# FoX/mLSTM/PEER encoder step: the forget sums of the later attention move from a product of their own into a 65th row of the keys

## The reference

```python
def fox_attend(q, F_q, q_pos, k, v, F_k):
    s = jnp.einsum('blhd,bshd->bhls', q, k).astype(jnp.float32) * (A_HEAD_DIM ** -0.5)
    s = s + F_q[..., None] - F_k[:, :, None, :]
    mask = jnp.arange(k.shape[1])[None, :] <= q_pos[:, None]
    p = jax.nn.softmax(jnp.where(mask, s, NEG), axis=-1).astype(v.dtype)
    return jnp.einsum('bhls,bshd->blhd', p, v)
```

## Time and profile before

| | |
|---|---|
| median of 3 runs | 4564.17 us (4562.99 to 4566.83) |
| profiled execution | 4577.09 us, span 4575.2 us |
| granted TensorE clock, mean | 0.86 |
| PE busy | 3507.8 us (77%) |
| DVE busy | 3136.7 us (69%) |
| POOL busy | 1793.7 us (39%) |
| ACT busy | 773.3 us (17%) |
| DMA | 1227 MB, 268 GB/s over the span |

### The profile page before, as it was taken

How to read it: one execution, slowest core, us unless ns; L and a number is a source line. 1 busy time by engine, 2 the same in 40 slices (tenths; PEclk the granted TensorE clock), 3 DMA queues, 4 the chain that set the end, 5 groups by cost and what they waited for, 6 DMA issues and landing times.

```text
span 4575.2 us, 37157 instructions
## 1 busy us (share of the span) xinstructions
PE 3507.8 (77%) x11412; PEld 2052.7 (45%) x11412; DVE 3136.7 (69%) x6095; ACT 773.3 (17%) x1322; POOL 1793.7 (39%) x1567
## 2 busy tenths in 40 slices
PE   7767786895588656966649666799898989998970
PEld 2434554553363443534535356544444444444430
DVE  1132203111688887996779889788888888888896
ACT  1141001101230322122222134200000000000000
POOL 0000000000566664762212221366666666666664
PEclk9888697898799877987769878799999999999995
DMA  6102121234999887996457665799999999999996
GB/s 263 61 27 87 65 78 38 85 99 149 327 356 345 311 303 286 404 358 223 144 160 248 211 195 172 251 410 409 409 400 404 398 403 408 399 406 405 402 389 241
DMA packets 436027, 1227.29 MB, mean 268 GB/s; under 512 B 40188, under 2 KB 162172, under 8 KB 431748
## 3 DMA queue, kind: packets, MB, share of 16 engines
q0 software_dynamic: 221184, 805.40, 46.7%
q1 hardware_dynamic: 107648, 209.81, 13.1%
q10 hardware_dynamic: 107024, 210.04, 12.4%
HBM read 1158.71 MB, written 66.39 MB: 268 GB/s over the span
## 4 chain that ended last, share of the span: by engine, by line
DVE 21%; DMA 18%; PE 15%; issue 10%; POOL 9%; ACT 2%; SPq 0%; DVEq 0%; POOLq 0%; ACTq 0%
DMA expert_rows<-in_expert_u,expert_index 12%; POOL expert_rows L2792 9%; PE ps_all L2202 6%; DVE acc L3018 3%; DVE expert_rows L3002 2%; DVE keep L2474 2%; PE ps_all L1610 2%; PE ps_all L2225 1%; DVE half_index L2882 1%; PE ps_all L1861 1%; PE ps_all L2501 1%; DVE half_index L2879 1%; PE ps_all L1824 1%; DMA expert_rows<-in_expert_v,expert_index 1%; DVE half_best L2881 1%
## 5 line engine op out<-in xcount | busy, mean ns | idle before, releaser
L2792 POOL DMA_INDIRECT expert_rows<-in_expert_v,expert_index x768 | 891.0, 1160 | 926.6 <-DVE acc L3018 425.1
L2792 POOL DMA_INDIRECT expert_rows<-in_expert_u,expert_index x768 | 892.1, 1162 | 693.5 <-DVE acc L3018 278.5
L3002 DVE CUSTOM_DVE_ANT_0 expert_rows<-expert_rows,h_rows_sb 128x1024 f32<-128x1024 f32 x768 | 923.3, 1223 | 168.7 <-DMA expert_rows<-in_expert_u,expert_index 158.6
L3018 DVE SCALAR_TENSOR_TENSOR acc<-expert_rows,weights,acc 128x1024 f32<-128x1024 f32 x756 | 937.1, 1289 | 31.7 <-DMA expert_rows<-in_expert_v,expert_index 28.8
L2521 PE MATMUL ps_all<-branchT,side 128*128 128x512 f32 x1536 | 714.7, 617 | 109.8 <-DVE side L2486 109.5
L2512 PE MATMUL ps_all<-hT,branchT 128*128 128x384 f32 x2048 | 704.5, 499 | 54.8 <-ACT side L2456 40.4
L2512 PEld LDWEIGHTS ps_all<-hT,branchT 128*128 128x128 f32 x2048 | 398.2, 195 | 369.5 <-issue 141.1
L2521 PEld LDWEIGHTS ps_all<-branchT,side 128*128 128x128 f32 x1536 | 300.5, 198 | 481.8 <-issue 326.3
L2202 PE MATMUL ps_all<-hT,side 128*128 128x384 f32 x1152 | 393.6, 499 | 38.1 <-ACT hT L2283 20.9
L2202 PEld LDWEIGHTS ps_all<-hT,side 128*128 128x128 f32 x1152 | 223.5, 196 | 196.6 <-ACT hT L2283 21.5
L2501 PE MATMUL ps_all<-keep 128*128 128x128 f32 x768 | 150.8, 365 | 86.4 <-DVE keep L2474 57.3
(11 more groups left out here) (405 smaller groups left out, 4356.3 us busy)
## 6 DMA issues: line engine op xcount, KB each, us to landing
branchT<-in_expert_uT ACTq DMA_DIRECT2D x128, 512.0 KB, 7.1
branchT<-in_expert_vj ACTq DMA_DIRECT2D x128, 512.0 KB, 9.6
w_mod_ring<-in_w_mod SPq DMA_DIRECT2D x12, 2048.0 KB, 9.9
gate_rows<-branchT ACTq DMA_DIRECT2D x12, 2048.0 KB, 9.9
keep<-gate_rows ACTq DMA_DIRECT2D x32, 768.0 KB, 12.4
side<-in_w_blk SPq DMA_DIRECT2D x40, 512.0 KB, 6.0
expert_rows<-in_expert_u,expert_index POOLq DMA_INDIRECT x768, 12.7
expert_rows<-in_expert_v,expert_index POOLq DMA_INDIRECT x768, 11.2
```

Source lines behind the costliest of these rows:

```text
L2792: pool.indirect_dma_start(rows[:, r % ROWS, :], None, io[table], bass.IndirectOffsetOnAxis(ap=eidx[:, q % 3, k:k + 1], axis=0)).then_inc(r ...
L3002: dve.tensor_tensor_reduce(rows[:, r % ROWS, :], rows[:, r % ROWS, :], h2[:, :], 1.0, 0.0, ALU.mult, ALU.add, dot[:, j, k:k + 1]).then_inc ...
L3018: dve.scalar_tensor_tensor(own, rows[:, r % ROWS, :], wgt[:, j, k:k + 1], own, ALU.mult, ALU.add).then_inc(row_used, 1)
```

## The change

The forget sums become row 64 of each head's keys, and the queries get a row of ones there. Rows 65 to 127 of both are zeros. The product of `head_rows` with `negF` goes. The keys of a pair, before one tile of 128 rows, are now two (one a head) with 64 rows used, and take twice the columns; the queries move into the columns of `hbT` that the chunk's mLSTM fills later. Each pair is loaded with 7 transfers (before: 8 in chunk 0, 6 in chunk 1), among them one `negF` row for each head from SBUF. The memsets become four large ones in chunk 0 and one in chunk 1, and now SP waits for them before it loads the first two pairs, and PE doesn't. The planned cost of an attend beat in `side_beats` becomes 0.75 a tile plus 0.8.

```diff
--- before.py
+++ after.py
@@ -1700,8 +1700,9 @@
         self.haT, self.hbT = branchT[:, 0:4, :], branchT[:, 4:8, :]
         self.causal, self.causalT = masks[:, P:2 * P], masks[:, 2 * P:3 * P]
         self.head_rows = masks[:, 4 * P:12 * P].rearrange("p (h t) -> p h t", h=AH)
-        pair = lambda a: (a[:, 4:8, 0:2 * P], a[:, 0:4, 0:2 * P], a[:, :, 2 * P:3 * P])
-        self.pair = (pair(branchT), pair(hT))
+        own = slice(tiles[0] * P, tiles[0] * P + LW)
+        pair = lambda j, a: (self.hbT[:, 2 * j:2 * j + 2, own], a[:, :, 0:2 * P].rearrange("p (h n) t -> p h n t", h=2), a[:, :, 2 * P:3 * P])
+        self.pair = (pair(0, branchT), pair(1, hT))
         self.prob = side[:, 0:2 * SEQ].rearrange("p (j t) -> p j t", j=2)
         self.probT = side[:, 2 * SEQ:2 * SEQ + 1024].rearrange("p (j t) -> p j t", j=2)
         head = lambda at: (side[:, at:at + LW], side[:, at + LW:at + 2 * LW],
@@ -1719,6 +1720,8 @@
         at += LW
         assert at <= SIDE, at
         self.s = s
+        self.first = not earlier
+        self.BLANKS, self.BLANKED = (4, (4, 4)) if self.first else (1, (4, 5))
         self.den, self.inv, self.ghb = s.den[:, 0:NL], s.inv[:, 0:NL], s.ghb
         self.past = {**earlier.totals(), "c_stored": 0} if earlier else {name: 0 for name in self.COUNTED + self.ONCE}
 
@@ -1735,7 +1738,7 @@
         counts.update({name: self.batch_base(self.BEATS) + 1 for name in self.BY_BATCH})
         counts.update({name: self.MB for name in self.BY_TILE})
         counts.update({name: BH for name in self.BY_HEAD})
-        counts.update(blanked=4 * self.NL, tail=self.TAIL * BH, pair_loaded=2 * self.pair_parts(), head_loaded=2 * 64, ghb_loaded=16)
+        counts.update(blanked=self.BLANKS, tail=self.TAIL * BH, pair_loaded=2 * self.pair_parts(), head_loaded=2 * 64, ghb_loaded=16)
         return counts
 
     def of(self, b):
@@ -1756,33 +1759,33 @@
 
     def sync_pair(self, sp, p):
         q, k, v = self.pair[p % 2]
+        if p < 2:
+            sp.wait_ge(self.s.blanked, self.BLANKED[p])
         if p >= 2:
             sp.wait_ge(self.s.out_ready, self.past["out_ready"] + (p - 1) * self.U)
         loaded = self.s.pair_loaded[p % 2]
-        lo = self.own.start
+        n = (self.prefix + 1) // 2
         for hh in range(2):
             own = slice(hh * AD, (hh + 1) * AD)
-            for i in range(self.NL):
-                sp.dma_start(self.slot(q, hh, i)[own], self.q_rows[own, p, lo + i * P:lo + (i + 1) * P]).then_inc(loaded, 16)
-        n = (self.prefix + 1) // 2
-        sp.dma_start(k[:, 0:n, :], self.io["new_kT"][:, p, 0:2 * n * P].rearrange("p (n t) -> p n t", t=2 * P)).then_inc(loaded, 16)
+            sp.dma_start(q[0:AD, hh, :], self.q_rows[own, p, self.own]).then_inc(loaded, 16)
+            sp.dma_start(k[0:AD, hh, 0:n, :], self.io["new_kT"][own, p, 0:2 * n * P].rearrange("p (n t) -> p n t", t=2 * P)).then_inc(loaded, 16)
+            sp.dma_start(k[AD:AD + 1, hh, 0:n, :], self.negF[2 * p + hh:2 * p + hh + 1, 0:2 * n * P].rearrange("p (n t) -> p n t", t=2 * P)
+                         ).then_inc(loaded, 16)
         sp.dma_start(v[:, 0:self.prefix, :], self.io["new_v"][:, 0:self.prefix, p * P:(p + 1) * P]).then_inc(loaded, 16)
 
     def pair_parts(self):
-        return 16 * (2 * self.NL + 2)
-
-    def slot(self, q, hh, i):
-
-        n = hh * self.NL + i
-        return q[:, n // 2, n % 2 * P:(n % 2 + 1) * P]
+        return 16 * 7
 
     def vector_blank(self, dve):
 
-        for q, _, _ in self.pair:
-            for hh in range(2):
-                other = slice((1 - hh) * AD, (2 - hh) * AD)
-                for i in range(self.NL):
-                    dve.memset(self.slot(q, hh, i)[other], 0.0).then_inc(self.s.blanked, 1)
+        blank = lambda rows: dve.memset(rows, 0.0).then_inc(self.s.blanked, 1)
+        if self.first:
+            later = self.hbT[:, :, FIRST * P:SEQ]
+            blank(later[AD:P])
+            blank(self.pair[0][1][AD:P])
+            dve.wait_ge(self.s.blanked, 2)
+            dve.memset(later[AD:AD + 1], 1.0).then_inc(self.s.blanked, 1)
+        blank(self.pair[1][1][AD:P])
 
     def sync_head(self, sp, h):
         q, k, kb, vb = self.head[h % 2]
@@ -1810,8 +1813,6 @@
         def scores(b):
             p, hh, i, t = self.of(b)
             q, k, _ = self.pair[p % 2]
-            if b == 0:
-                pe.wait_ge(self.s.blanked, self.past["blanked"] + 4 * self.NL)
             if b % self.U == 0:
                 pe.wait_ge(self.s.pair_loaded[p % 2], self.past["pair_loaded"] + (p // 2 + 1) * self.pair_parts())
             if b >= 2:
@@ -1820,14 +1821,13 @@
             for lo in range(0, (t + 1) * P, 512):
                 n = min(512, (t + 1) * P - lo)
                 last = lo + n == (t + 1) * P
-                queries = self.slot(q, hh, i)
-                pe.matmul(out[:, lo:lo + n], self.head_rows[:, 2 * p + hh, :], self.negF[:, lo:lo + n], start=True, stop=False)
+                queries = q[:, hh, i * P:(i + 1) * P]
                 whole = n // 256 * 256
                 if whole:
-                    pe.matmul(out[:, lo:lo + whole].rearrange("p (n t) -> p n t", t=256), queries, k[:, lo // 256:(lo + whole) // 256, :],
-                              start=False, stop=whole == n and not last)
+                    pe.matmul(out[:, lo:lo + whole].rearrange("p (n t) -> p n t", t=256), queries, k[:, hh, lo // 256:(lo + whole) // 256, :],
+                              start=True, stop=whole < n or not last)
                 if whole < n:
-                    pe.matmul(out[:, lo + whole:lo + n], queries, k[:, (lo + whole) // 256, 0:n - whole], start=False, stop=not last)
+                    pe.matmul(out[:, lo + whole:lo + n], queries, k[:, hh, (lo + whole) // 256, 0:n - whole], start=True, stop=not last)
             pe.matmul(out[:, t * P:(t + 1) * P], ident, self.causal, start=False, stop=True).then_inc(self.s.scores_ready, 1)
 
         def turn_pair(p, g):
@@ -2545,7 +2545,7 @@
         beats.append((("blank", c), 0, 0, 2, 1))
         for b in range(8 * NL):
             t = tiles[b % NL]
-            beats.append((("attend", c), b, 1.1 * (t + 1) + 1.0, 0.4 + 0.14 * (t + 1), 2))
+            beats.append((("attend", c), b, 0.75 * (t + 1) + 0.8, 0.4 + 0.14 * (t + 1), 2))
         for b in range(BH * NL):
             beats.append((("memory", c), b, 7, 1.5, 4))
         beats.append((("last", c), 0, 14, 1.5, 4))
```

## The result

The changed kernel takes 4606.66 us (median of 4 runs, 4597.43 to 4613.43), the kernel before 4565.5 in the same comparison: a ratio of 1.0087 (95% interval 1.0066 to 1.0108), some 40 us slower. The forecast was 4568, no change, with a range of 4538 to 4600. The profiled execution has a span of 4595.5 us, 20 more than the profiled one of before.

What follows compares the result with a forecast made beforehand. VectorE's busy plus idle time was taken to set the experts phase, with transfers bounding its late dense stretch. Moving two units summed to 0; 6.4 + 2 + 11 - 15 = +4 us gave 4568 us, range 4538 to 4600.

Steps and rivals of the forecast that it cites:

- The frame: Experts phase: VectorE runs one program in order, so the phase's time is exactly its busy time plus its idle time.
- the dense stretch: Late units with dense experts: bound by transfers, staying about 1484 us long and starting some 100 us earlier.
- three plain units: Tail, ahead of the last gelu: three units without dense experts instead of one, 48.8 us each.
- the sum: Whole kernel: blanks 6.4, start 2, chunk 0 idle 11, chunk 1 idle -15, together +4 us.
- The product: Attention scores: one matmul fewer per 512 columns, 61 us less PE work, counting only through VectorE's waits.
- The blanks and the start: Start of attention: memsets add 6.4 us of VectorE busy time; loads waiting for them add 2 us of waiting.
- Chunk 0: Its attention stretch: 99 us at an overlap of 1.6, VectorE idle 18 against 6.8, so +11 us.
- Chunk 1: Its attention stretch: 110 us at an overlap of 1.50, VectorE idle 20 against 35.6, so -15 us.
- rival 3: Chunk 1's attention: less PE work leaves the clock at 1.2 GHz, +10 to +20 us; 0.32 together with rival 2.
- Idle time in attention: Both attention stretches: VectorE's idle time from the overlap of VectorE and PE, +11 us in chunk 0, -15 in chunk 1.
- Rival 2: Front bound by the PE and ScalarE side chain: +45 us, 4609, cut to a third, 4583; 0.32 with rival 3.
- Rival 1: Attention: VectorE's 36.8 us of score waits beside the starts mostly go, -29 us, 4535; half, 4554; chance 0.30.

Runs made afterwards that it cites:

- e1: The changed kernel with the planned cost of an attend beat put back to 1.1(t+1)+1.0: 4561.4 us, 0.9985 of the kernel before.
- e7: The changed kernel with attend beats at their old planned cost and merge beats planned at 10.55 and 10.75 instead of 16.4: 4657.2 us.
- e5: The changed kernel with the planned cost of an attend beat raised to 1.45(t+1)+1.2: 4578.9 us, 1.0021 of the kernel before.
- e8: e1 with pair 0's queries, keys and values loaded before SP waits for the blanks: 4549.0 us, 0.9955 of the kernel before.

## Why the prediction was wrong

**The frame held.** VectorE's busy plus idle time describes the phase, the dense stretch stayed at 1485 us (69 us earlier, not the 100 said), three plain units came at 48.5 us each (said: 48.8). The front lost its two units of work and kept more idle time than said: +31.3 us where the sum had 2 + 11 - 15 = -2. Busy time gave 8.4 us where the sum had 6.4, and 3.2 us of idle time came behind the front.

**The product.** Removed as said. VectorE's waits show its worth: 17 us on the old plan, 33 on the new.

**The blanks and the start.** The rows add to 2.19 + 1.76 + 2.19 + 1.76 = 7.9 us, as said, but with gaps of 0.37, 0.59 and 0.38 us between them, so that SP's first load went out 9.3 us after the first memset began, not 8.1. The first scores wait 15.0 us (said 12.7), since the last transfer was issued at 1490.21 and PE's first product came at 1501.1; in e1 it is 11.5. The 12.7 came out of two slips: 1500.5 + 4.2 + 5.8 is 1510.5 and not 1514.5, and VectorE is ready 5.9 us later than before (7.9 less the 2.0 of the old blanks), at 1502.6 and not 1504.6. With e1 the window of the start measured +9.0 against 5.9 + 2 = 7.9 of the sum. The Trainium skill (VectorE: DVE Perf Modes, "Zero memsets can be issued as uint32") has one cycle an element, by an estimate at its 0.96 GHz 1.04 ns. The row of 2560 elements gives 2.19 us, 0.86 ns each; from its start to the start of the next memset it is 2.57 us, 1.00 ns each. So the price by the row was too low for what the four memsets took in sequence, and whether the gap belongs to the memset isn't shown. The working also says that norm to turn keeps three half-units; by `side_beats` it has four (23 to 26), and `turn` now shares a half-unit with the first attend beats of chunk 1. Their wait came out at 25.5 us against 27.0, so this cost nothing.

**Chunk 0.** Said: 99 us, VectorE 81, overlap 1.6, idle +11. Measured: 104.3 us, VectorE 88.4, PE 80.6, so an overlap of 1.62 and 15.9 us idle against 6.8: +9. The idle time was right; VectorE had 7 us more to do there than said.

**Chunk 1: the first term that failed.** Said: 110 us, overlap kept at 1.50, idle -15. Measured: 123.0 us, VectorE 88.4, PE 83.5, overlap 1.40, idle 34.5 against 35.6: -1. That is 14 us of the miss. I had given chunk 0 a lower overlap because its filler leaves, and kept chunk 1's, whose filler leaves too. The clock there was 0.77 against 0.79, so rival 3 has no visible share.

**"Idle time in attention": the term that wasn't there.** I worked out idle time for attention and set every other beat at no change, although the plan packs `out`, `norm` and the picks into other half-units too. About 19 us of the 31 lie there (31.3 less 9 of chunk 0 and 4.3 of the start, plus the 1 that chunk 1 gave): 7.6 in the merge, 9 in the output beats (13.9 and 3.8 against 8.6), 5 in the norm (11.7 against 6.8), less what smaller ones give back. This term, which the sum put at nothing, and the 14 us of chunk 1 are the miss.

**Rival 2 came nearest.** It was priced at +45 us, 4609: the front 61 us shorter and the tail 97.6 longer, measured 54.4 and 96.6. The forecast then cut it to a third because VectorE's work and PE's came out nearly equal in attention. The test was the wrong one: nearly equal sums over a stretch don't make a stretch without waits. The beats wait on each other in turn, so the two engines reached an overlap of 1.40 and 1.62 here and not 2, and much of the filler taken away turned into waiting. e7 shows the same with merge beats mostly in place of attention. That rival 2's number fits so closely is in part luck: it named chunk 0's attention as the place, which has 9 us of the loss, and 19 lie outside attention; and e5 shows that its chain isn't the only limit, since units put back beyond the old plan cost time instead of giving it.

**Rival 1** came true only with the plan left alone: 37 us of waits fell to 21, and e1 stands 7 us below the kernel before.

## What to carry to other kernels

When side work is spread over a bound engine's own work by planned costs, those costs don't say how long the side work takes, but how much of the bound engine's work is kept beside it. Making a step faster and then telling the planner so can give away more than the step saved; change the work first, time it, and move the plan as an edit of its own, in both directions. And when a move of beats is priced, every wait of the bound engine in the moved region is priced, not only that of the edited beats.

## What I hadn't expected

- The same two units moved cost 47 us packed by attention and 92 packed by merge (e7 against e1), so how many units move doesn't set the price. A likely reason, not tested by itself: PE's products for a merge beat take 15.5 us back to back (before, 1797.00 to 1812.48) against 10.55 planned in e7, while an attend beat took 4.1 us against 4.55 planned in the changed kernel.
- A plan of costs 1.6 times what a beat needs wasn't slack. In e1's window VectorE is busy 53.7 of 54.4 us with attend beats planned at 6.5 us for 5 tiles, where the dense stretch after shows one every 4.1 us (1587.5 to 1608.0, five beats).
- SP's wait ahead of loads that didn't need it cost twice what e1 kept of the shorter product (7 us): 14 us between e1 and e8 (7 to 21), of which 6 are seen in the start's window and the rest isn't placed.
